# Convolution and gate projections for block 0 ahead of the rows, and for blocks 1 to 3 between block 0's rows, in a one-core decoder layer

## What is computed

```python
z = x @ w_in                      # 9 sections of 1024: q f i og | conv B C h | gate_a gate_b
o_A = hgrn2_chunkwise(q, k, v, logf)                     # 8 heads, chunks of 64
yc = cb * causal_depthwise_conv3(cc * ch, conv_w, conv_b)
merged = sigmoid(ga) * (o @ w_branch_a) + sigmoid(gb) * (yc @ w_branch_b)
x = layer_norm(ALPHA * x + merged @ w_out)
# PEER: 8 heads, two top-16 searches, 16 experts of 16384 a head and token
h = gelu(einsum('thkd,td->thk', u[eidx], x));  y = einsum('thk,thkd->td', g * h, v[eidx])
x = layer_norm(ALPHA * x + y)
x = x + sigmoid(x @ w_gate) * (p @ w_proj)
```

## Time and profile before

| | us |
|---|---|
| median of 3 runs | 1983.08 (1982.08 to 1983.52) |
| the profiled execution | 1979.64 |
| its span | 1977.9 |
| TensorE matmul busy | 1738.5 (88%) |
| VectorE busy | 1159.2 (59%) |
| ScalarE busy | 827.1 (42%) |
| GpSimd busy | 492.3 (25%) |
| DMA | 632.83 MB, mean 320 GB/s |

### The profile page before, as it was taken

How to read it: one execution, slowest core, us unless ns; L and a number is a source line. 1 busy time by engine, 2 the same in 40 slices (tenths; PEclk the granted TensorE clock), 3 DMA queues, 4 the chain that set the end, 5 groups by cost and what they waited for, 6 DMA issues and landing times.

```text
span 1977.9 us, 18619 instructions
## 1 busy us (share of the span) xinstructions
PE 1738.5 (88%) x5700; PEld 981.6 (50%) x5700; DVE 1159.2 (59%) x2622; ACT 827.1 (42%) x2030; POOL 492.3 (25%) x531
## 2 busy tenths in 40 slices
PE   8999999999799999579999997889787779877787
PEld 6888788889655556234444442233222224322223
DVE  4454444321357778776646666676666676666653
ACT  6566532231242233534434444445444444444432
POOL 0000000000123233233223333333333333333330
PEclk9999999999899999699999999999999999999998
DMA  6112213136699999999989999999999999999992
GB/s 234 63 47 82 85 65 127 45 133 208 234 422 377 388 417 419 384 400 421 383 333 389 413 415 421 422 385 409 423 421 421 421 407 384 411 421 422 421 421 104
DMA packets 88212, 632.83 MB, mean 320 GB/s; under 512 B 9920, under 2 KB 10432, under 8 KB 12480
## 3 DMA queue, kind: packets, MB, share of 16 engines
q0 software_dynamic: 73728, 536.90, 66.3%
q1 hardware_dynamic: 14400, 94.93, 13.0%
HBM read 629.70 MB, written 2.10 MB: 319 GB/s over the span
## 4 chain that ended last, share of the span: by engine, by line
PE 51%; DMA 26%; ACT 10%; DVE 8%; issue 4%; POOL 0%; ACTq 0%; DVEq 0%; SPq 0%; POOLq 0%
DMA uv<-in_pk_uv,idx 25%; PE psum L1379 21%; PE psum L1166 15%; PE psum L1310 6%; PE psum L1352 4%; DVE uv L1044 4%; PE psum L1407 3%; ACT diag L687 1%; ACT coef L679 1%; ACT L675 1%; ACT w_hi L491 1%; DVE state L816 1%; ACT L655 1%; PE psum L1324 1%; PE psum L1210 1%
## 5 line engine op out<-in xcount | busy, mean ns | idle before, releaser
L1379 PE MATMUL psum<-uv,diag 128*128 128x512 f32 x1904 | 932.0, 619 | 202.7 <-ACT diag L687 192.3
L1044 DVE CUSTOM_DVE_ANT_0 uv<-uv,psum 128x1024 f32<-128x1024 f32 x512 | 624.1, 1219 | 399.8 <-DMA uv<-in_pk_uv,idx 394.5
L479 POOL DMA_INDIRECT uv<-in_pk_uv,idx x512 | 488.8, 955 | 1442.3 <-PE psum L1379 768.1
L1379 PEld LDWEIGHTS psum<-uv,diag 128*128 128x128 f32 x1904 | 343.9, 193 | 730.2 <-ACT diag L687 415.9
L675 ACT ACTIVATE gelu<-dots 128x1 f32<-128x1 f32 x512 | 103.3, 202 | 680.9 <-DVE dots L1044 676.1
L1166 PE MATMUL psum<-xTh,w_hi 128*128 128x512 f32 x576 | 231.2, 401 | 10.0 <-DVE xTl L842 9.6
L1166 PE MATMUL psum<-xTl,w_hi 128*128 128x512 f32 x576 | 225.6, 392 | 0.0
L1166 PE MATMUL psum<-xTh,w_lo 128*128 128x512 f32 x576 | 225.4, 391 | 0.0
L770 DVE TENSOR_TENSOR w_lo<-raw,w_hi 128x1024 fp32r<-128x1024 f32 x72 | 88.2, 1226 | 210.6 <-ACT w_hi L491 210.6
L687 ACT ACTIVATE diag<-ident,coef 128x128 f32<-128x128 f32 x476 | 191.2, 402 | 15.6
L679 ACT ACTIVATE coef<-gelu,weight 128x1 f32<-128x1 f32 x512 | 150.9, 295 | 16.7
(11 more groups left out here) (160 smaller groups left out, 1212.9 us busy)
## 6 DMA issues: line engine op xcount, KB each, us to landing
raw<-in_w_in SPq DMA_DIRECT2D x36, 1024.0 KB, 4.8
raw<-in_pk_w_q SPq DMA_DIRECT2D x16, 1024.0 KB, 4.8
raw<-in_w_branch_a SPq DMA_DIRECT2D x8, 1024.0 KB, 4.7
raw<-in_w_branch_b SPq DMA_DIRECT2D x8, 1024.0 KB, 7.0
raw<-in_w_out SPq DMA_DIRECT2D x8, 1024.0 KB, 4.8
uv<-in_pk_uv,idx POOLq DMA_INDIRECT x512
w_gate<-in_ple_w_gate SPq DMA_DIRECT2D x1, 4096.0 KB, 21.1
x_raw<-in_x_t SPq DMA_DIRECT2D x4, 512.0 KB, 7.5
```

The lines of the kernel that those rows point to most:

```text
L479: pool.indirect_dma_start(uv[:, r % UV, :], None, pk_uv, bass.IndirectOffsetOnAxis(idx[:, i % 2, j:j + 1], 0)).then_inc(row_in[r % UV], 16)
L1044: V.tensor_tensor_reduce(u, u, x_cur[:], 1.0, 0.0, ALU.mult, ALU.add, dots[:, r % 32:r % 32 + 1]).then_inc(dot_done, 1)
L1379: last = T.matmul(B[i][:], diag[:, n % DR, :], uv[:, r % UV, D + i * 512:D + (i + 1) * 512], start=(k == 0), stop=(k == BLOCK_ROWS - 1), s ...
```

## The change

**Ahead of the rows**, the convolution and gate sections are projected for block 0 alone, and the other way round: the 128 tokens are the stationary operand and 512 columns of w_in stream past (`z_tile`). Ten tiles (`Z_PARTS`) of 24 matmuls, each in four quarters (`zh` on ScalarE, `zl` on VectorE, four buffers `zw_hi`, `zw_lo`), with two 1 MB loads a tile. Results lie with tokens on partitions. u = C * h and B are turned (`turn_tok`) for the convolution along time (`conv0`, which keeps the last two tokens in `carry`), and `branch0` and `out0` work on the token side, the mix being turned once (`mix_turn`).

**Between block 0's rows**, the same sections are projected for blocks 1 to 3 (384 tokens) in 40 units of 24 matmuls, over rows 9 to 60 (`UNIT_ROW`), 18 or 19 matmuls a row, with `unit_hi` on ScalarE at the row where the unit two before ends (`HI_ROW`), `unit_lo` on VectorE at the top of the next row (`LO_ROW`), and the unit's reader one row after its end. Merge moves to rows 61 to 80, out to 83 to 93, norms to 96, 98 and 100, turns to 99, 101 and 103, queries to 105 and on.

**Rows' v half.** SHARED has 75 rows instead of 36: all up to row 93 but the 19 rows of 9 to 60 with r % 8 in (2, 5, 7).

**Data.** Only block 0's x is loaded early; x of blocks 1 to 3 comes after the last unit, over w_hi and w_lo, which lie outside the ring now. ln1's gain and bias lie in gaT and gbT's block 0 part; ln2's bias is loaded after block 0's fin_sum; w_ple after the last w_lo; w_gate after the last norm; keysT after the last out0; acc in oT's block 0 part. w_in's convolution and gate sections are read twice: 20 MB more.

The diff's core, with in this order the tiles, the schedule, SHARED, SP's loads, ScalarE's `unit_hi`, VectorE's row loop, and TensorE's `z_tile` and its `tail_row` (which follows `sum_v(r)`):

```diff
+        Z_PARTS = [(CHH, 0), (CC, 0), (CB, 0), (CHH, 1), (CC, 1), (CB, 1), (GA, 0), (GA, 1), (GB, 0), (GB, 1)]
...
+        UNITS = [(sect, 2 * cp + i) for cp in range(KT // 2) for sect in (6, 5, 4) for i in range(2)]
+        UNITS += [(sect, 2 * cp + i) for sect in (7, 8) for cp in range(KT // 2) for i in range(2)]
+        UNIT_MM = 3 * KT
+        QUERY0_ROW = {h: 2 * (h - 4) for h in range(4, PKH)}
+        UNIT_ROW = [[9 + (UNIT_MM * n + i) * 52 // (UNIT_MM * len(UNITS)) for i in range(UNIT_MM)] for n in range(len(UNITS))]
+        UNIT_END = [rows[-1] for rows in UNIT_ROW]
+        HI_ROW = [6, 7] + UNIT_END[:-2]
+        LO_ROW = [7, 8] + [t + 1 for t in UNIT_END[:-2]]
+        MERGE_ROW = [61 + n * 20 // 128 for n in range(16 * KT)]
+        OUT_ROW = [83 + n * 11 // 96 for n in range(4 * (TB - 1) * KT)]
+        NORM_ROW = [None] + [OUT_ROW[-1] + 1 + 2 * b for b in range(1, TB)]
+        TURN_ROW = [None] + [NORM_ROW[b] + 3 for b in range(1, TB)]
...
-        SHARED = [r for r in range(14, 104) if r % 5 in (1, 3)]
+        SHARED = [r for r in range(OUT_ROW[-1] + 1) if not (9 <= r <= 60 and r % 8 in (2, 5, 7))]
...
+            for m, (sect, q) in enumerate(Z_PARTS):
+                for i in range(2):
+                    if m < 2:
+                        sp.wait_ge(lo_done, unit_a(HEADS - 1, 2 * m + i) + 1)
+                    else:
+                        sp.wait_ge(zl_done, ZQ * (m - 1))
+                    fetch(w_in[sect, 2 * q + i], "z", m, i)
...
+            for n in range(len(UNITS) // 2):
+                if n < 3:
+                    sp.wait_ge(t_done, USE["query", 0, PKH - 3 + n, 1] + 1)
+                else:
+                    sp.wait_ge(ul_done, 2 * (n - 3) + 2)
+                sect, c = UNITS[2 * n]
+                fetch(w_in[sect, c // 2], "unit", n)
...
+            def unit_hi(n):
+                act.wait_ge(*loaded("unit", n // 2))
+                if n >= 2:
+                    act.wait_ge(t_done, USE["unit", n - 2] + 1)
+                nc.scalar.activation(w_hi[:, n % 2], raw[:, SLOT["unit", n // 2], :, (n % 2) * P:(n % 2) * P + P],
+                                     ACT.Copy).then_inc(uh_done, 1)
...
             for r in range(ROWS):
+                for n in range(len(UNITS)):
+                    if r == LO_ROW[n]:
+                        unit_lo(n)
                 dot(r)
...
+            def z_tile(m):
+                r = USE["z", m]
+                t_free(r)
+                for kq in range(ZQ):
+                    n = ZQ * m + kq
+                    pe.wait_ge(zl_done, n + 1)
+                    for k2 in range(KT // ZQ):
+                        k = KT // ZQ * kq + k2
+                        for i, (xx, w) in enumerate(((xTh, zw_hi), (xTh, zw_lo), (xTl, zw_hi))):
+                            last = T.matmul(B[bank(r)][:], xx[:, k, 0:P], w[n % 4][:, k2, :], start=(k == 0 and i == 0),
+                                            stop=(k == KT - 1 and i == 2))
+                    last.then_inc(t_done if kq == ZQ - 1 else zk_done, 1)
...
             def tail_row(r):
+                for n in range(len(UNITS)):
+                    for i in range(UNIT_MM):
+                        if r == UNIT_ROW[n][i]:
+                            unit_mm(n, i)
```

More of the change, by code:

```diff
@@ new lines, in build @@
+        LOADS += [(("branch0", n, i), 2 * (n % 2) + i) for n in range(4) for i in range(2)]
+        LOADS += [(("out0", n, i), 2 * n + i) for n in range(2) for i in range(2)]
+        LOADS += [(("query", 0, h), h % 3) for h in range(PKH)]
+        LOADS += [(("unit", n), (PKH + n) % 3) for n in range(len(UNITS) // 2)]
+        LOADS += [(("merge", m), m % 2) for m in range(8)]
+        LOADS += [(("out", c), c % 2) for c in range(4)]
+        LOADS += [(("query", 1, h), h % 2) for h in range(PKH)]
@@ L309, in blocks, with loaded @@
+        SLOT = dict(LOADS)
+        def loaded(*name):
+            names = [n for n, slot in LOADS if slot == SLOT[name]]
+            return raw_in[SLOT[name]], 16 * (names.index(name) + 1)
         def blocks(pc):
             return range(*PIECES[pc])
[L312 to L317, removed]
@@ L318, in build, with use @@
-        USE = {name: n for n, name in enumerate(USES)}
-        BY_VECTOR = ("merge", "out")
+        USES, BANK = [], []
+        def use(bk, *name):
+            USES.append(name)
+            BANK.append(bk)
+        for m in range(len(Z_PARTS)):
+            if m == 4:
+                use(3, "ut", 0)
+            if m == 5:
+                use(6, "cbt", 0)
+            if m == 7:
+                use(7, "ut", 1)
+            if m == 8:
+                use(4, "cbt", 1)
+            if m == 9:
+                use(5, "branch0", 0)
+            use(Z_BANK[m], "z", m)
@@ new lines, in build @@
+        use(6, "branch0", 1)
+        use(7, "branch0", 2)
+        use(4, "branch0", 3)
+        for kh in range(2):
+            use(5 + kh, "mixt", kh)
+        use(7, "out0", 0)
+        use(4, "out0", 1)
+        for kh in range(2):
+            use(5 + kh, "turn", 0, 0, kh)
+        rest = [("query", 0, h, i) for h in range(PKH) for i in range(4)]
+        rest += [("unit", n) for n in range(len(UNITS))]
+        rest += [("merge", 1, c, i) for c in range(4) for i in range(4)]
+        rest += [("out", 1, c, b) for c in range(4) for b in blocks(1)]
@@ new lines, in build, with by_vector_engine @@
+        rest += [("turn", 1, b, kh) for b in blocks(1) for kh in range(2)]
+        for n, name in enumerate(rest):
+            use(4 + (n + 3) % 4, *name)
+        for h in range(PKH):
+            for i in range(4):
+                use(4 + i % 2, "query", 1, h, i)
+        USE = {name: n for n, name in enumerate(USES)}
+        def by_vector_engine(u):
+            if u[0] == "z":
+                return Z_PARTS[u[1]][0] == CC
+            if u[0] == "unit":
+                return UNITS[u[1]][0] in (CC, CB)
+            return u[0] in ("ut", "cbt", "branch0", "out0", "merge", "out")
@@ L363, in _ @@
                     load(j, A_SECT[j], hp)
[L364 to L373, removed]
@@ L408, in _ @@
+            for c in range(4):
+                tail_fetch(8 + c, w_out[c], "out", c)
             ov = out.rearrange("a (b p) d -> p (a b) d", p=P)
@@ new lines, in unit_mm @@
+            def unit_mm(n, i):
+                k, i3 = divmod(i, 3)
+                r = USE["unit", n]
+                if i == 0:
+                    pe.wait_ge(ul_done, n + 1)
+                    t_free(r)
+                w, xx = ((w_hi, xTh), (w_lo, xTh), (w_hi, xTl))[i3]
+                last = T.matmul(B[bank(r)][:, 0:SEQ - P], w[:, n % 2, k, :], xx[:, k, P:], start=(i == 0),
+                                stop=(i == UNIT_MM - 1), skip_group_check=True)
+                if i == UNIT_MM - 1:
+                    last.then_inc(t_done, 1)
```

761 lines of the change are left out of this document (453 added, 308 removed).

## The result

The changed kernel takes **2039.62 us** (2038.98 to 2039.90, 4 runs) against 1983.3 us of the kernel before beside it (1982.08 to 1984.69, 4 runs): a ratio of 1.0283 [1.0265, 1.0301], 2.8% slower. The forecast was 2006 us, 1.2% slower. The direction was right, and so was the place of the stalls. The loss is 56 us where 23 were forecast: the time is 34 us above the forecast. The profiled execution took 2038.98 us, its span is 2036.9 us, 59.0 more than before.

The account below looks back on a forecast made before the run. TensorE was taken to bound the kernel before the first dot, DMA block 0's rows after it. 1977.9 - 154 + 6 + 132 + 21 + 17 + 1 = 2000.9 us of span, 2006 us as time; forecast range 1972 to 2040.

Parts of the forecast that it names:

- two signs of being wrong: The prediction is wrong if rows 9 to 60 take under 230 us, or the first dot is later than 402.
- the ring: Rows 9 to 60: w_hi waits for TensorE, w_lo precedes the dot, V rows wait for diag; stalls 50 and 42 us.
- All four wait in turn: Rows 9 to 60: no engine is late next, TensorE, VectorE, ACT and DMA each wait; 295 us in all.
- a few stretches at the half clock: Rows 9 to 60: small clock term that takes the sum from 291 to 295 us.
- rival B: Rows 9 to 60: stalls halve TensorE's clock for half of 199 us of matmuls, some 50 us more, 2050; chance 0.10.
- clock 0.99 after 1044.3: Earlier trace, rows after 1044.3: granted clock 0.99 although TensorE is busy only 750 of 898 us.
- 7 us of head 7's matmuls and branch0(0) between the tiles: Lead-in: TensorE work between z tiles, 7 us, part of the sum that ends z tile 9 at 317.
- 6.5 us a tile: Lead-in: loads, four ACT copies and the last subtraction take 13.0 us for two z tiles, longer than TensorE's 5.45.
- Rival D: Lead-in shrinks less because z tiles' loads queue: 9.6 us a tile, 31 us more, 2037; chance 0.05.
- 6 us a V row: Rows 40 to 60: sigmoid table loads make w_hi later, so seven V rows stall 6 us each, 42 us.
- no drain beside it: ScalarE, rows 40 to 60: a table load costs 1.28 us without the drain that would add 44 us over 32 switches.
- Rival A: Rows 9 to 60: the stalls don't form, 215 us there, 1926 in all; chance 0.20.

Follow-up runs that it names:

- e2: Changed kernel with TensorE's sum_v of the 19 V rows in rows 9 to 60 two rows later: 1960.59 us, ratio 0.9887.
- e7: Changed kernel with VectorE's dot ahead of w_lo in a row instead of behind it, no lag on TensorE: 1980.04 us.
- e1: Changed kernel with 14 small identity matmuls ahead of each of the 19 V rows' waits in rows 9 to 60: 2014.13 us, ratio 1.0154.
- e8: Changed kernel without the loads of z tiles 2 to 9, which reuse the weights of tiles 0 and 1: 2036.75 us.
- e9: Changed kernel with VectorE's w_lo of z quarters 20 and 21 ahead of head 7's last two operations and block 0's first convolution: 2036.75 us.
- e4: Changed kernel with Copy instead of Sigmoid for the gates of blocks 1 to 3 (rows 40 to 60): 2030.83 us.
- e5: As e2, and ScalarE copies w_hi ahead of its row's gelu instead of behind it: 1930.46 us, ratio 0.9735.
- e3: Changed kernel with all rows up to 93 in SHARED, so VectorE adds them and TensorE has no V row there: 1959.14 us, ratio 0.9854.
- e10: Changed kernel with V rows one row later on TensorE and w_hi ahead of the row's gelu on ScalarE: 1958.02 us.

## Why the prediction was right or wrong, point by point

**What was forecast and what came.** Neither of the prediction's two signs of being wrong appeared: rows 9 to 60 took more than 230 us, and the first dot came ahead of 402. Two terms of the sum were too small, and they hold the 36 us of the table above.

**Right: the ring and its size.** "50 us" for rows 9 to 39 was 51.6; "42" for rows 40 to 60 was 34.0; 92 in all against 85.6, in 19 waits. "All four wait in turn" was three in a ring, with GpSimd behind VectorE. e2 (no wait for diag, 81 us less) and e7 (w_hi and w_lo out of the chain, half the wait gone) show that the chain followed through the earlier trace rows is the cause. The interval of the 384-column matmul, 0.173, came out exactly, as did the V row's 1.72.

**Wrong: the term "a few stretches at the half clock", put at 4 us.** It measured 28.9 (e1). I had the mechanism as rival B, with its price of 50 and a chance of 0.10, and treated it as a separate case. It is not separate: in the changed kernel's trace the waits that I summed to 92 us bring it along, and only its size was open. (B's own sum was loose too: half of 199 us at half clock is 100 us more, and what of it hides wasn't worked out. The count above makes it 35.) What misled me was the reading "clock 0.99 after 1044.3": there TensorE is idle 148 us over 351 V rows, 0.4 us a row, and only three of its waits are longer than 2 us, while the earlier trace rows already showed what a V row does after a pause of several us, 3.78 for 1.72. The nearer row was the one to size from: 19 V rows with the surcharge of the earlier trace rows, 2.1 us, are 39 us: above the measured 29, but far nearer than 4. The Trainium skill (TensorE: Matmul & The Clock Gate, HAM oscillation — how this bites in real kernels) describes short bursts of matmuls with waits for DMA in between, which bring the clock down each time. The trace agrees in this, though the waits here are for another engine: 16 pieces at half clock, 85.3 us in all, with TensorE busy 73% of the stretch.

**Wrong: the lead-in, 388 against 400.6.** The failed step is the term "7 us of head 7's matmuls and branch0(0) between the tiles". The same paragraph has 7 us for one branch0 alone. From the start of z tile 0 at 240.8 to the end of z tile 9 at 329.8 TensorE's time, by starts, is:

| part | measured | forecast |
|---|---|---|
| ten z tiles (5.6 each at full clock, 56; the rest is mostly half clock) | 59.6 | 65, with the next row |
| waits for VectorE's w_lo: 2.6, 4.7, 0.5, 2.0 | 9.7 | |
| head 7's matmuls 6.7, turns 2.2, branch0(0) 8.5 | 17.4 | 7 |
| wait for branch0's load | 2.5 | 5 |
| sum | 89.0 | 77 (318, put at 317) |

So 10 of the 12.6 us are matmuls between the tiles that the sum left out. "6.5 us a tile" came near the measured 6.9 by luck: it was the pace of loads, copies and one subtraction, and e8 shows that the loads don't set the pace. What fills it up beside TensorE's own 5.6 is half clock and VectorE: the waits at 280.9 and 305.4 come from VectorE's other work in the tiles' path, the convolution above all (e9's rows, and the chain's first three lines). The wait at 313.1 is branch0's load (the chain's DMA line). Rival D's price (31) was more than twice the miss, and its mechanism, queued loads, isn't what happened.

**Sized too high: ScalarE's table loads in the gates' part.** 6 us a V row was 4.9 (34.0 by 7), and e4 shows the loads' share of the stretch at 13 us. Two switches in the changed kernel's trace, with ScalarE's instructions around them:

```profile
646.60 0.29 ACT L789 ACTIVATE coef<-gelu,weight 128x1 f32<-128x1 f32 x1
646.91 1.28 ACT L742 ACT_TABLE_LOAD   x1
648.21 0.49 ACT L742 ACTIVATE gaT<-psum 128x384 f32<-128x384 f32 x1
648.72 1.28 ACT L785 ACT_TABLE_LOAD   x1
650.01 0.20 ACT L785 ACTIVATE gelu<-dots 128x1 f32<-128x1 f32 x1
```

Each load starts 0.02 us after the instruction before it ends, and the next instruction 0.01 to 0.02 us after the load's end. So the step "no drain beside it" holds. The load of 1.28 us agrees with the Trainium skill (ScalarE: Activation LUTs, What ACT_TABLE_LOAD costs); its 2.7 us a switch isn't seen here, neither in these rows nor in e4, where 27 loads fewer are worth 13 us.

**Right: what follows.** Rows 61 to 93 and 94 to 127 are within 2 us, with TensorE busy 120.4 of 128.9 us and DMA at a share of 0.96 in the first, so that neither alone is shown to be its bound, and DMA at 0.99 in the second. Row 128 on took 0.4 us less than before, well inside the 7 us by which that part varies; a cost of the new ln2_bias load isn't seen.

**Rival A** was priced at 215 us for rows 9 to 60 and 1926 in all. e5 took 210.8 and 1930.46: the price was right, and so was the reason why the change doesn't get it. Its order of instructions ties TensorE to VectorE in the row itself, and nothing else in the kernel had to be given up to untie it. That the whole time agrees so well is in part luck: in e5 the first dot comes 9.0 us later than the forecast's and rows 61 to 93 take 4.5 more, while rows 0 to 60 and those from 94 on take 9.4 less.

**Still open.** Why e2 and e3, with different clocks (0.96 and 0.90) and sums, end at the same 239 us was read from their waits, not tested beyond e5. e10's return of the waits could be w_hi delaying its own row's diag by 1.06 us, or TensorE running faster into it; no run tells these apart.

## What to carry to other kernels

When independent work is interleaved with a pipeline on engines that are strictly in order, follow one turn of the pipeline across all queues and ask at each place what the waiting instruction holds up: here two lines (the consumer two rows later, the producer of the next weights ahead of a wait for this row) turned a change of +2.8% into -2.65%, with not one instruction less. Price waits of several us on TensorE twice, once as time and once as half clock afterwards, from the nearest row that shows one. Give every matmul between two others a term of its own. And before a load's pace is taken as the bound of a stretch, add up the engine's own work in it, gaps of its feeders included.

## What the runs showed of the hardware that was not expected

- A wait of 2.0 to 6.2 us, 4.5 in the mean, about every 17 us (19 in 320.7) was enough for TensorE to spend 85.3 of 320.7 us at 1.2 GHz while it was busy 73% of the time. With the waits filled by 14 identity matmuls each, it was 10.2 of 291.8 us.
- The work that suffers most here is what comes right behind the wait: 53 of the 76 V instructions ran at half clock (0.853 us), but only 84 of the 939 unit matmuls in the trace.
- A change of activation table cost ScalarE the load of 1.28 us and 0.02 us on either side of it, no more (646.91 and 648.72 us).
